# First MLP product of two token groups as seven block products, their hidden rows through DRAM

## The reference, cut to what matters

```
def sq_relu_mlp(h, w1, w2):
    return jnp.square(jax.nn.relu(h @ w1)) @ w2

h = rms_norm(x, norm_g[2]) * (1 + sc2) + sh2
x = x + gt2 * rms_norm(sq_relu_mlp(h, w1, w2), norm_g[3])
```

## Time and profile before

| | |
|---|---|
| Median of 3 runs | 2832.82 us (2831.36 to 2833.03) |
| Span of the profiled execution | 2831.4 us |
| Time of an execution around its span | some 1.4 us (median less span) |
| PE busy | 2746.3 us, 97% |
| DVE, ACT, POOL busy | 1467.5, 1268.5, 194.9 us |
| Granted TensorE clock | 0.8 of full speed in the first of 40 slices, 0.9 or more in all others |
| DMA | 355.5 MB, 126 GB/s over the span |

### The profile page before, as it was taken

The page is one execution under the profiler, slowest core; times in us unless marked ns, Lnnn a source line. Parts: engine busy times, 40 slices in busy tenths (PEclk is TensorE's granted clock), DMA queues, the critical chain, the costliest instruction groups (busy, mean ns, idle before and its releaser), DMA issues.

```text
span 2831.4 us, 39609 instructions
## 1 busy us (share of the span) xinstructions
PE 2746.3 (97%) x15219; PEld 2422.2 (86%) x15219; DVE 1467.5 (52%) x2230; ACT 1268.5 (45%) x2078; POOL 194.9 (7%) x180
## 2 busy tenths in 40 slices
PE   5999999999999999999999998889999999999998
PEld 3878888889999999999998887777899999999997
DVE  4256666555545544544512558985645454445444
ACT  5134445554434434433423676764544343334333
POOL 0000000000000000000000008970000000000000
PEclk8999999999999999999999999999999999999999
DMA  7642322634434434444313451025344343434343
GB/s 269 208 151 97 105 85 81 193 114 126 125 121 149 126 123 129 143 125 126 117 49 100 145 170 38 1 97 186 112 126 126 120 149 126 126 126 149 126 126 111
DMA packets 301845, 355.53 MB, mean 126 GB/s; under 512 B 22246, under 2 KB 244908, under 8 KB 300684
## 3 DMA queue, kind: packets, MB, share of 16 engines
q1 hardware_dynamic: 295472, 335.92, 37.4%
q10 hardware_dynamic: 4220, 9.86, 1.0%
q0 software_dynamic: 2016, 7.86, 0.8%
HBM read 338.27 MB, written 15.34 MB: 125 GB/s over the span
## 4 chain that ended last, share of the span: by engine, by line
PE 87%; DVE 4%; ACT 4%; issue 2%; DMA 1%; SPq 1%; POOL 0%; ACTq 0%; DVEq 0%; POOLq 0%
PE ps L2159 38%; PE ps L2237 27%; PE ps L1973 8%; PE ps L2293 4%; PE ps L1934 2%; PE ps L2027 1%; PE ps L2054 1%; PE ps L2393 1%; PE ps L1990 1%; DVE t_g L1604 1%; ACT junk_n L1010 1%; ACT prT L943 1%; SPq L540 1%; ACT ps L1271 1%; DVE p_lo L1415 1%
## 5 line engine op out<-in xcount | busy, mean ns | idle before, releaser
L1415 DVE TENSOR_TENSOR p_lo<-p_raw,p_hi 128x1024 fp32r<-128x1024 f32 x507 | 622.1, 1229 | 644.4 <-ACT p_hi L854 643.3
L854 ACT ACTIVATE p_hi<-p_raw 128x1024 fp32r<-128x1024 f32 x507 | 532.9, 1053 | 516.7 <-DMA p_raw<-mlp_w 412.0
L2237 PE MATMUL ps<-hm_hi,p_hi 128*128 128x384 f32 x1536 | 515.6, 336 | 0.8 <-DVE p_lo L1415 0.8
L2237 PE MATMUL ps<-hm_hi,p_lo 128*128 128x384 f32 x1536 | 515.9, 336 | 0.0
L2237 PE MATMUL ps<-hm_lo,p_hi 128*128 128x384 f32 x1536 | 514.5, 335 | 0.0
L2159 PE MATMUL ps<-p_hi,hid_hi 128*128 128x512 f32 x1152 | 362.7, 396 | 3.3 <-DVE p_lo L1415 3.3
L2159 PE MATMUL ps<-p_lo,hid_hi 128*128 128x512 f32 x1152 | 357.3, 391 | 0.0
L2159 PE MATMUL ps<-p_hi,hid_lo 128*128 128x512 f32 x1152 | 356.5, 391 | 0.0
L1064 ACT ACTIVATE relu<-ps 128x384 f32<-128x384 f32 x192 | 94.4, 492 | 541.7 <-PE ps L2237 541.7
L1647 DVE TENSOR_TENSOR sqr<-relu 128x384 f32<-128x384 f32 x192 | 107.1, 558 | 392.4 <-ACT relu L1064 392.3
L2237 PEld LDWEIGHTS ps<-hm_hi,p_hi 128*128 128x128 f32 x1536 | 288.4, 188 | 9.8 <-DVE p_lo L1415 2.5
(11 more groups left out here) (248 smaller groups left out, 3680.0 us busy)
## 6 DMA issues: line engine op xcount, KB each, us to landing
p_raw<-mlp_w SPq DMA_DIRECT2D x384, 512.0 KB, 3.9
mod_p<-mod_w SPq DMA_DIRECT2D x80, 512.0 KB, 3.9
p_raw<-gla_w_in SPq DMA_DIRECT2D x56, 512.0 KB, 3.5
p_raw<-gla_w_out SPq DMA_DIRECT2D x24, 512.0 KB, 3.2
mod_w<-mod_w SPq DMA_DIRECT2D x8, 1024.0 KB, 18.9
p_raw<-ab_w_in SPq DMA_DIRECT2D x14, 512.0 KB, 5.1
p_raw<-ab_w_out SPq DMA_DIRECT2D x24, 256.0 KB, 4.3
p_raw<-ab_w_out SPq DMA_DIRECT2D x12, 512.0 KB, 3.5
```

The source lines that it names most:

```text
L854: nc.scalar.activation(p_hi[s][:, :, 0:width], p_raw[s][:, :, 0:width], ACT.Copy).then_inc(pan_hi, 1)
L1415: V.tensor_tensor(p_lo[s][:, :, 0:width], p_raw[s][:, :, 0:width], p_hi[s][:, :, 0:width].bitcast(F32), ALU.subtract).then_inc(pan_lo, 1)
L2237: mm = M.matmul(ps[:, b, 0:GN], w[s][:, c, :], x[:, c, :], start=(c == 0 and x is hi and w is p_hi), stop=(c == DC - 1 and w is p_lo))
```

## The change

Groups 1 and 2 no longer have `up` and `down` steps of their own. Group 0 runs as before (32 steps, fully unrolled). Then come 16 *jobs* per layer. A job takes 256 hidden features (two row blocks) and the 768 tokens of both groups (two column blocks), and splits the sum over 1024 inputs into two halves of 512 (`CC` = 4 chunks). Its 2x2x2 blocks make eight block products; the changed kernel computes the four output blocks from seven products of sums and differences of blocks (`PRODUCTS`, Winograd's form of Strassen's scheme). One block product is 4 chunks x 3 terms = 12 matmuls of 384 columns.

- Token side, once per layer: sums of token blocks, made by DVE and ACT in group 0's steps 18 to 29 from the turned chunks (`turn_second`, `sum_seconds`, `split_seconds`): two DVE operations of 1536 elements per row and four of 768, then four splits and four roundings of 1536.
- Weight side, per job: one DMA of 1 MB (`pair_in`), four sums of 128x512 on DVE (`sum_weights`), seven roundings on ACT (`round_piece`), seven lo parts on DVE (`split_piece`). Pieces lie in the panel ring, in eight half slots.
- Output side, per job: one copy on ACT (`copy_p1`), five sums with a PSUM bank on DVE (`sum_block`), four relus on ACT (`relu_block`), four squares on POOL (`square_blocks`), four stores of 192 KB to DRAM (`hid_scratch`). Banks 0 to 2 and 3 to 5 alternate between jobs.
- Group 0's three post steps stand in jobs 0 and 1.
- Then 64 second products follow each other, group 1's 32 and group 2's 32. Each loads its w2 panel and its hidden block from DRAM (`held_in`, 192 KB), ACT rounds it and DVE splits it (two steps ahead). Between group 1 and group 2 stand group 1's post steps.
- Several pairs of semaphores are merged into one, and some waits with them. The hardware loops are gone.

```diff
+PIECES_HELD = 2 * SLOTS
+PRODUCTS = 7
+JOBS = FF // (2 * P)
...
+    io["hid_scratch"] = nc.dram_tensor("hid_scratch", ((GROUPS - 1) * NF, P, GN), F32, kind="Internal").ap()
...
+        C_BLOCKS = ((0, 0), (1, 1), (1, 0), (0, 1))
+        SECOND = tuple(c + CC * k for c in range(CC) for k in range(2))
...
+        def raw_piece(j, step):
+            return (w_block(j, 0, 0), w_sum[1][:], w_sum[0][:], w_block(j, 1, 0), w_block(j, 0, 1), w_block(j, 1, 1),
+                    w_sum[1][:])[step]
+        def sums_before(step):
+            return (0, 2, 1, 3, 0, 0, 4)[step]
+        def piece_slot(j, step):
+            return (PRODUCTS * j + step) % PIECES_HELD
+        def c_bank(j, which):
...
+            return 3 * (j % 2) + which
...
+        def second_operand(layer, step, x, c):
+            if step in (0, 4):
+                return hm[layer][1][x][:, c + (CC if step else 0), :]
+            if step == 6:
+                return b22[layer][x][:, c, :]
+            i = {2: 0, 1: 1, 3: 2, 5: 3}[step]
+            if x == 0:
+                return t_hi[layer][i][:, c, :]
+            n = CC // len(t_lo[layer][i])
+            return t_lo[layer][i][c // n][:, c % n, :]
...
+                for f in range(NF):
+                    up(f)
+                    if f:
+                        down(f - 1)
                 down(NF - 1)
+                def pair_in(j):
+                    sp.dma_start(w_pair[j % 2][:], w1_pairs[j]).then_inc(w_in[j % 2], 16)
+                def block_out(j, k):
+                    row, g = C_BLOCKS[k]
+                    sp.wait_ge(c_squared, 4 * JOBS * layer + 4 * j + k + 1)
+                    sp.dma_start(hid_d[NF * g + 2 * j + row], c_out[k][:]).then_inc(hid_out[k], 16)
+                def held_in(n):
+                    g, f = divmod(n, NF)
+                    k = C_BLOCKS.index((f % 2, g))
+                    sp.wait_ge(hid_out[k], HID_BASE + 16 * (JOBS * layer + f // 2 + 1))
+                    sp.dma_start(hq_raw[layer][n % 4][:], hid_d[n]).then_inc(hq_in[n % 4], 16)
+                sp.wait_ge(up_done[1], NF // 2 * (layer + 1))
+                pair_in(0)
+                pair_in(1)
+                start = PRODUCTS * JOBS * layer
+                for j in range(JOBS - 1):
+                    if j + 2 < JOBS:
+                        sp.wait_ge(piece_lo, start + PRODUCTS * (j + 1))
+                        pair_in(j + 2)
+                    for k in range(4):
+                        block_out(j, k)
+                last_job = start + PRODUCTS * (JOBS - 1)
+                for n in range(4):
+                    sp.wait_ge(product, last_job + 2 * n + 1)
+                    down(n)
+                    if n == 0:
+                        sp.wait_ge(product, last_job + 2)
+                        held_in(0)
+                        held_in(1)
+                        held_in(2)
+                        held_in(3)
+                    if n:
+                        block_out(JOBS - 1, n - 1)
+                block_out(JOBS - 1, 3)
+                for n in range(4, HELD_ROWS):
+                    down(n % NF)
+                    held_in(n)
...
+            def square_blocks(layer):
+                for n in range(4 * JOBS):
+                    pool.wait_ge(c_relu, 4 * JOBS * layer + n + 1)
+                    nc.gpsimd.tensor_tensor(c_out[n % 4][:], c_out[n % 4][:], c_out[n % 4][:], ALU.mult).then_inc(c_squared, 1)
+            square_blocks(0)
...
+            def round_piece(layer, j, step):
+                n = PRODUCTS * j + step
+                if n < PIECES_HELD:
+                    act.wait_ge(pan_used, SLOTS + FEEDS_TO_PAIRS[layer] - SLOTS + n // 2 + 1)
                 else:
-                    if f == 0:
+                    act.wait_ge(product, PRODUCTS * JOBS * layer + n - PIECES_HELD + 1)
+                if step == 0:
+                    act.wait_ge(w_in[j % 2], W_BASE + 16 * (JOBS // 2 * layer + j // 2 + 1))
+                if sums_before(step):
+                    act.wait_ge(w_summed, 4 * (JOBS * layer + j) + sums_before(step))
+                nc.scalar.activation(w_hi[layer][piece_slot(j, step)][:], raw_piece(j, step), ACT.Copy).then_inc(piece_hi, 1)
+            def copy_p1(layer, j):
+                n = JOBS * layer + j
+                act.wait_ge(product, PRODUCTS * n + 1)
+                if n:
+                    act.wait_ge(c_relu, 4 * n - 1)
+                nc.scalar.activation(c_sum[0][:], ps[:, c_bank(j, 0), 0:GN], ACT.Copy).then_inc(p1_copied, 1)
+            def relu_block(layer, j, k):
+                n = JOBS * layer + j
+                if n:
+                    act.wait_ge(hid_out[k], HID_BASE + 16 * n)
+                if k == 0:
+                    act.wait_ge(product, PRODUCTS * n + 5)
+                    x = ps[:, c_bank(j, 0), 0:GN]
+                else:
+                    act.wait_ge(c_summed, 5 * n + (0, 3, 4, 5)[k])
+                    x = c_sum[(0, 2, 0, 1)[k]][:]
+                nc.scalar.activation(c_out[k][:], x, ACT.Relu).then_inc(c_relu, 1)
+            def round_held(layer, n):
+                act.wait_ge(hq_in[n % 4], HQ_BASE + 16 * (HELD_ROWS // 4 * layer + n // 4 + 1))
+                nc.scalar.activation(hq_hi[layer][n % 4][:], hq_raw[layer][n % 4][:], ACT.Copy).then_inc(hq_rounded, 1)
+                panel_hi()
+            def pairs(layer):
+                for step in range(PRODUCTS):
+                    round_piece(layer, 0, step)
+                for j in range(JOBS):
+                    for step in range(PRODUCTS):
+                        if step == 0:
+                            if j:
+                                relu_block(layer, j - 1, 3)
+                            copy_p1(layer, j)
+                        if step == 4:
+                            relu_block(layer, j, 0)
+                            relu_block(layer, j, 1)
+                        if step == 6:
+                            relu_block(layer, j, 2)
+                        if j + 1 < JOBS:
+                            round_piece(layer, j + 1, step)
+                        elif step in (3, 5):
+                            round_held(layer, step // 2 - 1)
+                        if (j, step) in ((0, 0), (0, 4), (1, 3)):
+                            post_square(layer, 1, 0, ((0, 0), (0, 4), (1, 3)).index((j, step)))
+                relu_block(layer, JOBS - 1, 3)
...
+            def sum_weights(layer, j, i):
+                n = 4 * (JOBS * layer + j)
+                made = PRODUCTS * (JOBS * layer + j)
+                if made and i in (0, 1):
+                    dve.wait_ge(piece_lo, made - (4, 0)[i])
+                if i == 3:
+                    dve.wait_ge(piece_lo, made + 2)
+                if i == 0:
+                    dve.wait_ge(w_in[j % 2], W_BASE + 16 * (JOBS // 2 * layer + j // 2 + 1))
+                elif i == 1:
+                    dve.wait_ge(w_summed, n + 1)
+                out, x, y, op = ((w_sum[0][:], w_block(j, 1, 0), w_block(j, 1, 1), ALU.add),
+                                 (w_sum[1][:], w_sum[0][:], w_block(j, 0, 0), ALU.subtract),
+                                 (w_block(j, 1, 0), w_block(j, 0, 0), w_block(j, 1, 0), ALU.subtract),
+                                 (w_sum[1][:], w_block(j, 0, 1), w_sum[1][:], ALU.subtract))[i]
+                V.tensor_tensor(out, x, y, op).then_inc(w_summed, 1)
+            def split_piece(layer, j, step):
+                n = PRODUCTS * (JOBS * layer + j) + step
+                dve.wait_ge(piece_hi, n + 1)
+                i = piece_slot(j, step)
+                V.tensor_tensor(w_lo[layer][i][:], raw_piece(j, step), w_hi[layer][i][:].bitcast(F32),
+                                ALU.subtract).then_inc(piece_lo, 1)
+            def sum_block(layer, j, i):
+                n = JOBS * layer + j
+                dve.wait_ge(product, PRODUCTS * n + (2, 4, 4, 6, 7)[i])
+                if i == 0:
+                    dve.wait_ge(p1_copied, n + 1)
+                    if n:
+                        dve.wait_ge(c_relu, 4 * n)
+                if i == 2:
+                    dve.wait_ge(c_summed, 5 * n + 2)
+                b = ps[:, c_bank(j, 2 if i in (2, 4) else 1), 0:GN]
+                out, x = ((c_sum[1], c_sum[0]), (c_sum[2], c_sum[0]), (c_sum[2], c_sum[2]), (c_sum[0], c_sum[0]),
+                          (c_sum[1], c_sum[1]))[i]
+                V.tensor_tensor(out[:], b, x[:], ALU.add).then_inc(c_summed, 1)
+            def split_held(layer, n):
+                dve.wait_ge(hq_rounded, HELD_ROWS * layer + n + 1)
+                V.tensor_tensor(hq_lo[layer][n % 4][:], hq_raw[layer][n % 4][:], hq_hi[layer][n % 4][:].bitcast(F32),
+                                ALU.subtract).then_inc(hq_ready, 1)
+                panel_lo()
+            def pairs(layer):
+                for step in range(PRODUCTS):
+                    if step == 0:
+                        for i in range(3):
+                            sum_weights(layer, 0, i)
```

(74 more changed lines are left out.)

346 lines of the change are left out of this document (204 added, 142 removed).

## The result

The changed kernel takes 2781.68 us in the median of 4 runs (2780.66 to 2784.13), against 2832.93 (2831.36 to 2836.09) of the kernel before: ratio 0.9817, 95% interval 0.9803 to 0.9831. That is 51.3 us less; 44.7 were forecast. In a second session it was 2781.74 against 2833.81 us, ratio 0.9817 (0.9803 to 0.983).

A forecast was written before the change was run, and what follows sets the result against it. The MLP was taken as bound by TensorE's number of matmuls. Removing 384 saves 66.9 us; less 2 x (7.2 + 1.0 + 3.0 - 0.9) and 1.6, that is 44.7 us less: 2788.1 us, range 2774 to 2812.

The forecast's parts named there:

- posts in the jobs: waits: Start of jobs, per layer: third product 4.0 us late for group 0's post step, then 2.1 us of DVE backlog.
- posts in the jobs: lower clock: TensorE's clock falling after the stall at the jobs' start: 2 us at most, counted in the range only.
- end of the jobs: First second products wait for panels and for banks read by the last sums: 1.0 us per layer, bounds 0 and 4.
- group 1 to 2: Second-product stage: accumulators awaited openly while squared and scaled between the groups, 3.0 us per layer, bounds 2.5 and 4.
- old changes of group: Group changes in the kernel before: 0.45 us lost at each, twice per layer, 0.9 us per layer saved.
- steady jobs: Jobs of 14.63 us with DVE, ACT and POOL work fitting inside; 0.05 us extra booked per job, 1.6 for 32.
- second products in a row: 64 second products per layer at 4.12 us each if their operands come; priced at zero extra.
- Start of the jobs: Per layer: first product 1.1 us late, third 4.0, job 1's block sum 2.1; together 7.2, bounds 2.4 and 13.
- rival 4: Jobs: waits between short groups cost TensorE about 0.1 us each, 22 us more, 2811 us; chance 5%.
- margin before the fourth product: In each job DVE reads the second product's bank 0.7 us before the fourth product, which adds to it, starts.
- Rival 2: Jobs: DVE becomes the bound through POOL, a job some 15.5 us, 28 us back, 2817 us; chance 14%.
- The sign for a row stage: Stage of second products: the prediction is wrong if a row stage takes over 267 us.

The follow-up runs named there:

- Experiment 1: Changed kernel with each job's first block product computed twice, so as many matmuls as before the change: 2839.93 us beside 2834.41 of the kernel before.
- experiment 2: Changed kernel with group 0's three post steps left out of the jobs, signals kept: span 2764.6 us against 2778.9.
- experiment 3: Changed kernel with group 0's post steps moved earlier: span 2776.0 us; with DVE's weight sums and first split also behind the first block sum: 2768.7.
- Experiment 4: Changed kernel with two panels on each side of the group 1 to 2 border worked off tile by tile: span 2780.1 us; in a mended order 2780.4.
- experiment 5: Changed kernel with the jobs' squares on ACT instead of POOL: span 2786.6 us; with each square done twice on POOL: 2810.9.
- the mended tile order: Changed kernel, two panels at the group 1 to 2 border worked off by tiles, first panel's slot given back earlier than in the first try: span 2780.4 us.

## Why the prediction was right, and where it was off

**Direction, mechanism and range were right.** 2788.1 us were forecast and 2781.68 measured. Experiment 1 shows that the gain is the seven products in place of eight, and that all else together is a net loss. The terms of the sum, for both layers together:

| term | booked | measured | from |
|---|---|---|---|
| matmuls | -66.9 | -68.8 | 3072 x 0.1743 less 2688 x 0.1736 us |
| first product late | +2.2 | +1.6 | idle 0.86 and 0.78 |
| posts in the jobs: waits | +12.2 | +9.8 | experiment 2, less the next row |
| posts in the jobs: lower clock | 0 | +4.2 | 10 and 18 matmuls at 0.32 in place of 0.174 us |
| third product late without posts | 0 | +1.3 | idle 0.7 and 0.6 in experiment 2 |
| end of the jobs | +2.0 | 0 | chain at 1098.14 |
| group 1 to 2 | +6.0 | +6.3 | start at 1237.38, below |
| old changes of group | -1.8 | -1.8 | |
| steady jobs | +1.6 | 0 | 1224 matmuls without a hole |
| second products in a row | 0 | -3.9 | 4.085 in place of 4.12 us, 112 of them (16 more carry transposes) |
| sum | -44.7 | -51.3 | the MLPs' own: -51.5 |

**Start of the jobs.** The step holds in its parts: the load landed after 6.12 us (6.4 taken), tile 0's scaling ended at 865.57, 11.0 us after the landing (10.9), and the third product waited 3.8 us (4.0). The backlog behind it, 2.1 taken, shows as a wait of 1.5 and 1.6 us. So the waits were booked somewhat too high, and still the posts cost 6.4 and 7.6 us against 6.1. What was priced at nothing is the clock. The prediction named it, with 2 us at most, and put it in the range only; it fell in both layers, for 1.5 and 2.7 us. Without the posts, and with the reordered queues, it didn't fall. Experiments 2 and 3 show both parts to hang on the posts, and nearly all of it on where they stand in the queues.

**End of the jobs.** The 1.0 us per layer was a guess without a row, and was nothing: panels and rows were there.

**Group 1 to group 2.** 3.0 us from the post chain, and 3.1 measured: the first matmul on the last scaled tile starts at 1237.38; the row at 1231.06 and seven steps of 0.4535 us, the pace of the rows before it, would give 1234.2. Of these 3.1 us 2.4 are shown as idle; the rest lies in wider spacing right behind each wait. Experiment 4 shows that the cause is the scaling, and that hiding it costs slots. The granted clock didn't fall at these three short waits.

**The steady job.** No hole, and 0.1736 us per matmul, so rival 4 (0.1 us lost at every short group) falls as well. The margin before the fourth product is wider than the 0.7 us of the timetable: in the job from 1010.63 on, DVE has read the bank at 1015.54, the fourth product starts at 1016.87, margin 1.3. The prediction says that without the turns of DVE and POOL the margin would be 1.3 us; by its own timetable, which has holds of 0.4 and 0.9, it would be 2.0. A square alone lasts 0.8 us and not 0.9. The mean of 932 ns on the page contains its waits for DVE. Rival 2 had the mechanism (experiment 5) but not the weight; even a doubled square left the kernel 20 us faster than before.

**The sign for a row stage.** The prediction calls itself wrong if a row stage takes over 267 us. Layer 0's took 270.4 us and layer 1's 264.4. The limit was set wrongly: it forgets that 16 of layer 0's second products carry transposes (0.33 us each time, 4.45 us per product), as they did in before, so they are no cost of the change and not in the sum.

**What was missing.** Two small gains of the new stages were priced at zero: rows of one kind of matmul run a little faster than alternating ones, 4.085 us for 18 and 0.1736 for one block-product matmul against 4.12 and 0.1743. They are 5.8 us together; in the timeline of before the extra lies in the first matmuls behind each switch between the two forms. With the guessed 2.0 and 1.6 us of cost that did not come, and 0.6 at the first product, that is 10.0. From it go the posts' 1.8, the third product's 1.3 and 0.3 at the change of groups. That leaves 6.6 us, which is what the gain was underrated by. So the forecast was as near as it was partly by luck: errors of 10.0 and 3.4 us offset each other in part.

## What to carry to other kernels

Where TensorE is busy at 97% and an engine beside it at half, trading an eighth of a stage's matmuls for sums can pay: here 51.3 us of the 72.7 that the matmuls and their closer spacing are worth (68.8 and 3.9), and 66.4 with the queues and tiles reordered. The loss sits where stages meet, not in their steady part. At such a border look at the order of the helping engines' queues first: here 12 us vanished by placing the same instructions differently. And look at the granted clock behind every wait of TensorE of a few microseconds: here a wait of 3.8 us was followed by matmuls at the lower clock, which cost 1.5 and 2.7 us that no list of waits shows. A ring of slots that hides loads is part of that order: an edit that releases two slots together moves the wait instead of removing it.

## What the runs showed of the hardware that was not expected

Two operations of DVE and POOL that both read SBUF alternated when both queues were full: 1.13 to 1.31 us for a DVE operation of 0.68, 1.09 to 1.27 for a POOL operation of 0.83. Each square doubled, as two short operations, cost 0.8 us per job. The switch between 384-column and 512-column matmul groups, invisible as idle time, costs some 0.03 us each time by the two paces above.

The 13 traced executions differed by up to 4 us in the stage between the MLPs, which none of the edits touched. The length goes with the granted clock there. First the shortest, in after, then the longest, in the mended tile order:

```profile
1368.30:1987.00 618.70, 583.36 (x3073) 506.03 (x3072) 362.61 (x544) 346.02 (x566) 187.39 (x169) 1.00 0.32 99
1367.30:1990.00 622.70, 590.61 (x3074) 513.57 (x3073) 362.64 (x544) 346.17 (x566) 187.45 (x169) 0.98 0.31 99
```

The two executions with the least time at the lower clock took 618.7 and 619.0 us, the one with the most 622.7, and over all 13 the length and that time have a correlation of 0.92. Why the clock fell more often in some executions of the same instructions than in others is open.
